# High and low parts of the input side by side: one 512-column product with the high weights in place of two of 256

## The reference, cut to what matters

```python
# first block
z = rmsnorm(x, pre_mix_norm) @ w_in            # 2048 -> 3392, then convolution and attention
mix = concat([rmsnorm(u), rmsnorm(attn)]) @ w_out          # "out1", 2048 -> 2048
x = x + rmsnorm(mix, post_mix_norm)
hf = rmsnorm(x, pre_ffn_norm)
ff = (silu(hf @ w_gate) * (hf @ w_up)) @ w_down            # 2048 -> 5632 -> 2048
x = x + rmsnorm(ff, post_ffn_norm)
# second block
proj = rmsnorm(x, norm1_g) @ w_in_2            # "in2", 2048 -> 3072, pooling and recurrence
h = x + concat([y_pool, y_lru]) @ w_out_2                  # "out2", 2048 -> 2048
q = rmsnorm(h, norm2_g) @ peer_wq              # "wq": keys, top 16 of 128 x 128, experts
h = h + sum over 8 heads x 16 experts of gate * gelu(peer_u[e] . z) * peer_v[e]
return rmsnorm(h, norm_f_g)
```

## Time and profile before

| | |
|---|---|
| time, median of 3 runs (lowest to highest) | 2894.47 us (2893.43 to 2894.62) |
| the profiled execution, its own time | 2897.16 us |
| its span, first to last instruction | 2895.3 us |
| mean granted TensorE clock | 0.759 of full |
| busy: TensorE, VectorE, ScalarE, GpSimd | 1535.5, 2261.4, 694.4, 553.5 us |
| matmuls, weight loads | 11822, 11822 |

### The profile page before, as it was taken

The page is one execution under the profiler, slowest core; times in us unless marked ns, Lnnn a source line. Parts: engine busy times, 40 slices in busy tenths (PEclk is TensorE's granted clock), DMA queues, the critical chain, the costliest instruction groups (busy, mean ns, idle before and its releaser), DMA issues.

```text
span 2895.3 us, 31194 instructions
## 1 busy us (share of the span) xinstructions
PE 1535.5 (53%) x11822; PEld 1495.5 (52%) x11822; DVE 2261.4 (78%) x2771; ACT 694.4 (24%) x899; POOL 553.5 (19%) x619
## 2 busy tenths in 40 slices
PE   8998888999999999799994540000000000000000
PEld 8986788999999999789894540000000000000000
DVE  6974547554555455587758999999999999999998
ACT  5423444443443344445442200000000000000000
POOL 0000021000000000210002224343333333433331
PEclk9998898999999999899997765555555555555555
DMA  7542344555555555544558989999999999999997
GB/s 223 176 117 93 94 157 141 176 187 179 184 184 179 188 176 165 168 138 159 164 182 315 389 324 410 392 399 422 422 422 422 422 422 422 421 422 422 421 422 316
DMA packets 339319, 798.81 MB, mean 276 GB/s; under 512 B 23249, under 2 KB 270635, under 8 KB 273195
## 3 DMA queue, kind: packets, MB, share of 16 engines
q0 software_dynamic: 73728, 536.90, 44.9%
q1 hardware_dynamic: 265515, 260.96, 28.4%
HBM read 795.72 MB, written 2.10 MB: 276 GB/s over the span
## 4 chain that ended last, share of the span: by engine, by line
DVE 39%; issue 10%; PE 10%; ACT 1%; DVEq 0%; POOL 0%; POOLq 0%
DVE pl L2000 10%; DVE pg L2000 10%; DVE row L1984 10%; PE pl L734 3%; PE pl L730 3%; PE pl L731 3%; DVE wlo L1488 1%; DVE dots L1984 0%; DVE cand L1968 0%; DVE cand L1965 0%; DVE cposf L1971 0%; DVE xlo L1670 0%; DVE top_i L1935 0%; DVE top_i L1928 0%; DVE work L1929 0%
## 5 line engine op out<-in xcount | busy, mean ns | idle before, releaser
L1488 DVE TENSOR_TENSOR wlo<-raw,whi 128x1024 fp32r<-128x1024 f32 (+1 forms) x460 | 555.1, 1219 | 462.2 <-ACT whi L1049 457.9
L730 PE MATMUL pl<-xhi,whi 128*128 128x256 f32 x2720 | 677.1, 286 | 48.5 <-DVE xlo L1670 36.3
L731 PE MATMUL pl<-xlo,whi 128*128 128x256 f32 x2720 | 674.9, 285 | 0.0
L1049 ACT ACTIVATE whi<-raw 128x1024 fp32r<-128x1024 f32 (+1 forms) x468 | 483.6, 1041 | 597.2 <-PE pl L734 507.3
L730 PEld LDWEIGHTS pl<-xhi,whi 128*128 128x128 f32 x2720 | 528.1, 194 | 53.0 <-issue 41.9
L731 PEld LDWEIGHTS pl<-xlo,whi 128*128 128x128 f32 x2720 | 528.4, 194 | 0.1
L734 PE MATMUL pl<-xhi,wlo 128*128 128x256 f32 x2720 | 384.7, 284 | 2.4 <-DVE wlo L1488 2.4
L734 PEld LDWEIGHTS pl<-xhi,wlo 128*128 128x128 f32 x2720 | 353.7, 193 | 2.8 <-DVE wlo L1488 2.8
L660 POOL DMA_INDIRECT row<-in_peer_u,expert x256 | 239.9, 937 | 484.5 <-DVE expert L1973 167.9
L660 POOL DMA_INDIRECT row<-in_peer_v,expert x256 | 242.6, 948 | 373.8 <-DVE dots L1984 184.4
L2000 DVE SCALAR_TENSOR_TENSOR pl<-row,dots,pl 128x2048 f32<-128x2048 f32 x127 | 299.0, 2354 | 13.1
(11 more groups left out here) (287 smaller groups left out, 1575.3 us busy)
## 6 DMA issues: line engine op xcount, KB each, us to landing
raw<-in_w_in SPq DMA_DIRECT2D x50, 1024.0 KB, 5.3
raw<-in_w_gate SPq DMA_DIRECT2D x44, 1024.0 KB, 5.0
raw<-in_w_up SPq DMA_DIRECT2D x44, 1024.0 KB, 5.0
raw<-in_w_out SPq DMA_DIRECT2D x32, 1024.0 KB, 5.3
raw<-in_w_down SPq DMA_DIRECT2D x32, 1024.0 KB, 5.3
raw<-in_peer_wq SPq DMA_DIRECT2D x16, 1024.0 KB, 7.0
raw<-in_w_down SPq DMA_DIRECT2D x16, 768.0 KB, 4.6
raw<-in_w_ukv SPq DMA_DIRECT2D x4, 1024.0 KB, 5.1
```

Source lines behind the costliest of these rows:

```text
L730: mm(banks[f][:, 0:S], w, xh[:, x, :], start=(half == 0 and t == 0), stop=False)
L731: mm(banks[f][:, 0:S], w, xl[:, x, :], start=False, stop=False)
L1049: return nc.scalar.activation(o, i, ACT.Copy)
L1488: V.tensor_tensor(wlo[:, n % 4, 0:k, :], w[:, :, f, :], whi[:, n % 4, 0:k, :].bitcast(F32), ALU.subtract)\
```

## The change

The input's high and low parts, `xhi` and `xlo`, become one tensor `x_split` in which the low 256 columns of a tile follow its high ones; the hidden values `hhi` and `hlo` likewise become `h_split`. With `apart=True`, `half_group` issues one product of the high weights with all 512 columns. The low part's sum then lies in columns 256 to 511 of the bank; the product with the low weights goes on into columns 0 to 255. Whoever empties a bank adds its halves. An instruction reads only one half of a bank pair at a time, so there is one more step for each, and a semaphore between dependent steps. in1 and in2 pass `apart=False` and keep two products (on the new layout), and the queries are left as they are.

```diff
-        xhi = sb("xhi", "xhi", 0, [P, DT, S], F32R)
-        xlo = sb("xlo", "xlo", 0, [P, DT, S], F32R)
+        x_split = sb("x_split", "xhi", 0, [P, DT, 2, S], F32R)
+        xhi, xlo = x_split[:, :, 0, :], x_split[:, :, 1, :]
...
+        def parts(pair):
+            v = pl_all[:, pair * 1024:(pair + 1) * 1024].rearrange("p (f h s) -> p f h s", f=2, h=2)
+            return v[:, :, 0, :], v[:, :, 1, :]
...   half_group, TensorE
-                        mm(banks[f][:, 0:S], w, xh[:, x, :], start=(half == 0 and t == 0), stop=False)
-                        mm(banks[f][:, 0:S], w, xl[:, x, :], start=False, stop=False)
+                        if apart:
+                            mm(banks[f], w, xs[:, x].rearrange("p h s -> p (h s)"), start=first_product,
+                               stop=(half == 1 and t == k - 1), skip_group_check=True)
+                        else:
+                            mm(banks[f][:, 0:S], w, xs[:, x, 0, :], start=first_product, stop=False)
+                            mm(banks[f][:, 0:S], w, xs[:, x, 1, :], start=False, stop=False)
...   out1, ScalarE, then VectorE
-                    for a, fn, done in ((sq, ACT.Square, norm_sq), (dst, ACT.Copy, ready)):
-                        for f in range(2):
...
-                            last = activation(d, PAIRS[g % 2][f][:, 0:S], fn)
-                        last.then_inc(done, 1)
+                    copy(two_tiles(src, g, i), parts(g % 2)[0]).then_inc(copied, 1)
+                    act.wait_ge(ready, 3 + g if i is None else i * 2 + (3 + g))
+                    activation(two_tiles(sq, g, i), two_tiles(src, g, i), ACT.Square).then_inc(norm_sq, 1)
...
+                    dve.wait_ge(copied, 1 + g if i is None else i * 2 + (1 + g))
+                    d = two_tiles(dst, g, i)
+                    V.tensor_tensor(d, d, parts(g % 2)[1], ALU.add).then_inc(ready, 1)
...   gates: ScalarE (gate_out, ahead of the Silu), then VectorE (scale_gates)
+                    act.wait_ge(mul_ready, pairs + 1 if i is None else i + (pairs + 1))
+                    copy(silu[:], parts(0)[0]).then_inc(gate_copied, 1)
...
-                        last = V.tensor_tensor(silu[:, f, :], pl[f][:, 0:S], rstd[:], ALU.mult)
+                    V.tensor_tensor(silu[:], silu[:], parts(0)[1], ALU.add).then_inc(gate_summed, 1)
...
+                    V.tensor_tensor(silu[:], silu[:], both, ALU.mult).then_inc(gate_scaled, 1)
...   ups, VectorE (multiply)
-                        last = V.tensor_tensor(hid[:, f, :], silu[:, f, :], pl[2 + f][:, 0:S], ALU.mult)
+                    V.tensor_tensor(hid[:], silu[:], high, ALU.mult).then_inc(up_high, 1)
+                    V.tensor_tensor(silu[:], silu[:], low, ALU.mult).then_inc(up_low, 1)
+                    V.tensor_tensor(hid[:], hid[:], silu[:], ALU.add).then_inc(mul_ready, 1)
...   down and out2, VectorE (down_out shown; out2_out the same with res)
-                        last = V.tensor_copy(d, bank) if c == 0 else V.tensor_tensor(d, d, bank, ALU.add)
+                    last = V.tensor_copy(d, high) if c == 0 else V.tensor_tensor(d, d, high, ALU.add)
+                    last.then_inc(down_added, 1)
+                    V.tensor_tensor(d, d, low, ALU.add).then_inc(down_ready, 1)
```

More of the change, by code:

```diff
@@ L716, in wide_total, with half_group @@
                 mm(pnorm, ones[:], sq_sum[:, 1, :], start=False, stop=True).then_inc(norm_sum, 1)
-            def half_group(first, half, banks, xh=xhi, xl=xlo, k=KU, i=None, step=0, arriving=None):
+            def half_group(first, half, banks, xs=x_split, k=KU, i=None, step=0, arriving=None, apart=True):
                 for f in range(2):
@@ L955, in _ @@
             pe.wait_ge(in2_ready, 12)
-            group(PIECE0["in2b"] + 12, PAIRS[1])
+            group(PIECE0["in2b"] + 12, PAIRS[1], apart=False)
             for j in range(2):
@@ L1254, in layer @@
                 out(2 * turns - 1)
-            layer("out1", 4, out1_ready, tmp, mix)
+            layer("out1", 4, out1_copied, out1_ready, tmp, mix)
             weights_hi(UNIT0["gu0"], PIECE0["gu0"])
@@ L1688, in scale_gates @@
                     k = pairs + 1
[L1690 to L1694, removed]
-                        last = V.tensor_tensor(silu[:, f, :], pl[f][:, 0:S], rstd[:], ALU.mult)
-                    last.then_inc(gate_scaled, 1)
+                    dve.wait_ge(gate_copied, k if i is None else i + k)
+                    V.tensor_tensor(silu[:], silu[:], parts(0)[1], ALU.add).then_inc(gate_summed, 1)
+                    dve.wait_ge(gate_summed, pairs + 1 if i is None else i + (pairs + 1))
+                    V.tensor_tensor(silu[:], silu[:], both, ALU.mult).then_inc(gate_scaled, 1)
                 def multiply(at, i=None):
@@ L1706, in multiply @@
                     dve.wait_ge(hid_lo, k + 1 if i is None else i + (k + 1))
-                    for f in range(2):
-                        last = V.tensor_tensor(hid[:, f, :], silu[:, f, :], pl[2 + f][:, 0:S], ALU.mult)
-                    last.then_inc(mul_ready, 1)
+                    high, low = parts(1)
+                    V.tensor_tensor(hid[:], silu[:], high, ALU.mult).then_inc(up_high, 1)
+                    dve.wait_ge(up_high, k + 1 if i is None else i + (k + 1))
+                    V.tensor_tensor(silu[:], silu[:], low, ALU.mult).then_inc(up_low, 1)
+                    dve.wait_ge(up_low, k + 1 if i is None else i + (k + 1))
+                    V.tensor_tensor(hid[:], hid[:], silu[:], ALU.add).then_inc(mul_ready, 1)
                 def hidden_lo(at, i=None):
@@ L1885, in out2_out @@
                 dve.wait_ge(piece_used, pc + 4 * (g + 1) if i is None else i * 8 + (pc + 4 * (g + 1)))
-                for f in range(2):
-                    t = 2 * g + f
-                    r = res[:, t, :] if i is None else res[:, bass.ds(i * 4 + t, 1), :].rearrange("p a b -> p (a b)")
-                    last = V.tensor_tensor(r, r, pl[2 * (g % 2) + f][:, 0:S], ALU.add)
-                last.then_inc(out2_ready, 1)
+                r = two_tiles(res, g, i)
+                high, low = parts(g % 2)
+                V.tensor_tensor(r, r, high, ALU.add).then_inc(out2_added, 1)
+                dve.wait_ge(out2_added, g + 1 if i is None else i * 2 + (g + 1))
+                V.tensor_tensor(r, r, low, ALU.add).then_inc(out2_ready, 1)
                 dve.wait_ge(out2_ready, 2 + g + 1 if i is None else i * 2 + (2 + g + 1))
```

66 lines of the change are left out of this document (39 added, 27 removed).

## The result

| | before | after |
|---|---|---|
| time, median (lowest to highest), runs | 2893.95 us (2892.53 to 2894.62), 4 | 2876.76 us (2874.18 to 2877.54), 4 |
| the profiled execution | 2897.16 us | 2877.54 us |

The ratio is 0.9939, with a 95% interval from 0.9927 to 0.9951. The gain is 17.2 us where 27.5 were forecast; the time lies 10 us above the forecast of 2867: inside the wide range (2838 to 2902), and 0.8 us above the narrow one (2858 to 2876) that was given for the forecast's own mechanism.

The account below looks back on a forecast made before the run. TensorE was taken to bound the part until about 1540 us, where all changed products lie. 2897.16 - 34.4 + 6.8 = 2869.6 us profiled, 2867 us for the median; narrow range 2858 to 2876, wide 2838 to 2902.

Parts of the forecast that it names:

- the forecast's own mechanism: Changed products: each matmul instruction pays a constant 13.3 ns over its columns, so merging a pair saves it once; chance 0.50.
- The product, 0.2267 us: Merged 512-column matmul at full clock: 0.2133 us of columns plus 0.0133 us once, against 0.240 us for a pair.
- (a): Changed products: the 13.3 ns are the weight load's, 512 columns take 0.2158 us; gain 55 us, 2839 us; chance 0.13.
- (b): Changed products: cost grows with columns, 512 take 0.240 us; nothing gained, ends remain, 2901 us; chance 0.22.
- The argument from the earlier trace against (a): At 1389.95 us a matmul started 0.12 us after the last despite a load 0.05 us late, so loads don't set pace.
- The gain per pair, 13.3 ns: In out1, feed-forward and out2, each pair of 256-column products made one of 512 columns saves 13.3 ns.
- 2624 x 0.0133 = 34.9 us: Total TensorE gain over all 2624 merged pairs; 34.4 us after 0.5 us off for pairs at half clock.
- What lies beside other work: Loops: extra emptying on ScalarE and VectorE is hidden beside TensorE, some 4 us to spare at the gates.
- Rival (c): Loops: evictions reach the path, ScalarE's copy delays weights, some 20 us of 27.5 go, 2887 us; chance 0.15.
- The ends, 6.8 us: Longer emptying chains at stage ends: down starts 4.2 us together, out1 1.2, last down and out2 1.4.
- the sum without the counted savings: Cost of the stage ends if the products gain nothing: 6.3 us.
- The nothing elsewhere: Stages outside the changed products, such as pooling products and expert stage, were forecast to change by 0.

Follow-up runs that it names:

- The probe: Separate kernel, not an edit: TensorE alone issues weight loads and matmuls in stretches of one width and alternating widths; steady 512-column product 0.22665 us.
- 16-and-16 kernel: Changed kernel with the 512-column products of both pieces first, then both pieces' low-weight products; 2877.14 us, ratio 0.9941.
- two-products kernel: Changed kernel's layout and emptying, but two 256-column products again instead of one of 512; 2906.09 us, ratio 1.0037 to the kernel before.
- kernel with the old emptying: Changed kernel's 512-column products, banks emptied by the old code from columns 0 to 255 only, low input's half never added; 2869.34 us, ratio 0.992.
- kernel with shorter ends: Changed kernel with ScalarE copying the up banks' high half and VectorE scaling silu earlier, leaving add and multiply behind; 2873.68 us, ratio 0.9931.
- both profiles of before: The kernel before, unedited, profiled a second time beside its first profile; 2893.16 us for the second, 2897.16 us for the first.
- in2 kernel: Changed kernel with shorter ends and sixteen wide, then sixteen narrow products, plus in2's groups on 512-column products; 2870.78 us, ratio 0.9921.

## Why the prediction was right, and where its sizes were off

- **The product, 0.2267 us: right.** The probe has 0.22665. Rivals (a) and (b) fall with it, and the change has this distance from the sixth wide product of a piece on. The argument from the earlier trace rows against (a) was misread, though. The matmul at 1389.95 was recorded on time, but it lasted 0.32 us instead of 0.28, and the next one started 0.158 us behind it by single starts, instead of 0.120:

```profile
1390.10 0.40 PE L734 MATMUL pl<-xhi,wlo 128*128 128x256 f32 x2
```

  So the load that came 0.05 us late did hold the stream up, by nearly 0.04. A load has some 10 ns to spare beside 256 columns, an estimate from these rows that fits the probe (0.1116 where the load seems to set the pace, against 0.120). The conclusion was right; what shows it is the probe, not the row.
- **The gain per pair, 13.3 ns: mis-sized, 10.8 measured.** The step that failed is "2624 x 0.0133 = 34.9 us". It took the steady price for all products, while each piece changes its width twice, and that costs 20 ns per 8 pairs (6 in the third down product), some 2.5 ns a pair: 2624 x 0.0025 = 6.6 us of the 7.2 that the changed stages lack. Rows of before could not show it, having one width. The probe and the 16-and-16 kernel show it each by itself. Why a change of width costs this, and what the 13.3 ns of the steady run are, no run shows.
- **What lies beside other work: right.** No gap in the loops with 14% more VectorE work; the two-products kernel has the old 184.32 us. Rival (c) is out for these stages.
- **The ends, 6.8 us: right.** Forecast 1.3, 1.3 and 1.6 for the down starts; the shorter chain takes back 1.4, 1.4 and 2.0. With the products unchanged all ends, the 0.2 of the norm among them, cost 6.3 us, and 6.3 was the sum without the counted savings. In the change they are 6.8 against the kernel with the old emptying, without out2's end, and 7.4 by subtraction: 34.9 - 0.5 - 6.6 = 27.8, and the stages gave 20.4.
- **The nothing elsewhere: not quite.** The pooling products took 1.4 us longer. There TensorE has waited 2.0 us for VectorE, in this kernel as in before, and its clock then stood at half for 3.4 us in the change but not in the kernel with shorter ends (windows of the stage):

```profile
1357.40:1368.40 11.00, 8.71 (x34) 6.60 (x33) 8.93 (x18) 3.99 (x4) 0.00 (x0) 0.86 0.00 0
```
```profile
1354.40:1364.00 9.60, 7.31 (x34) 5.81 (x32) 8.88 (x18) 3.94 (x4) 0.00 (x0) 1.00 0.00 0
```

  The same work, clock 0.86 against 1.00. It was at full in both profiles of before and in four of the experiments, and partly at half in the last two. Right behind, TensorE waits for out2's input (4.3 us, and 5.2 with in2 changed too) and comes back to a clock at half; the first 7 us of out2 from there, of the change and of the kernel with shorter ends:

```profile
1384.60:1391.60 7.00, 6.66 (x24) 5.06 (x25) 6.26 (x12) 3.50 (x4) 0.00 (x0) 0.67 0.42 139
```
```profile
1380.10:1387.10 7.00, 6.12 (x19) 4.72 (x20) 6.02 (x11) 3.19 (x4) 0.00 (x0) 0.54 0.41 137
```

  Here the change has the higher clock, and its out2 is 1.3 us shorter than that kernel's 109.34: pooling and out2 together take 119.1 and 119.0 us. So this 1.4 is no loss of the edit; where the stretches at half clock fall against the work shifts a microsecond from one stage to the next. The expert stage took 1.9 us longer in the change's profile. VectorE's waits there that both profiles of before lack:

```profile
DVE pl L2031 <- DVE pl L2031: 0.9, 2, 0.5
DVE row L2015 <- DMA row<-in_peer_u,expert: 0.8, 1, 0.8
```

  The second is one row of experts that came late. The two-products and the in2 kernel have such a wait of 0.8 us too, two others 0.4 in all, the 16-and-16 kernel and the one with shorter ends none. The first, two steps some 0.35 us longer than usual, is in the profile of the change and of each of the six kernels built on its layout, and in neither of before. No run sought its cause, and it stays open, as does the rest of the 0.7 to 2.0 us that the expert stage takes longer in all of them.
- **The total.** 27.5 forecast; less 6.6 for the changes of width and 0.8 at the ends and the norm, 20.1; less 1.4 and 1.9 for pooling and experts, 16.8; 17.2 measured. The part ahead of out1 scatters by some 4 us, so the last microseconds can't be assigned, and that the two agree within 0.4 is in part luck.

## What to carry to other kernels

When a trace shows a fixed excess of each instruction over its columns, ask before counting on it whether it is paid per instruction, per column or per load, and whether alternating shapes pays something of its own: one probe of 160 us answers all of it. Merging two products by widening the free dimension moves work to the emptying; here that work cost nothing where TensorE bounded a loop, and 0.5 to 2 us at each place where a stage ended in a dependent chain. So shorten the chain behind the last product first, and leave the merge out of a stage where the emptying engine is awaited right behind, as in in2.

## What was not expected of the hardware

- In this operand form the excess is 13.3 ns for 256, 320, 384 and 512 columns and 20.0 ns for 448. Why 448 differs stays open.
- A run of 512-column products behind 256-column ones takes about 27 ns extra over its first five starts (233, 236, 228, 233, 230 against 226.65), and 7 ns come back on the first narrow ones (113 and 119 for 120). It was measured the same with idle neighbours and in the full kernel. The probe's 384-column products behind 512-column ones take as much extra (171, 175, 177, 185, 176, 182 against 173.3), its 448-column ones behind 384 none. What causes it was not shown.
- A column's price did not depend on whether the 512 lie in one run or in two of 256, nor on the bank.
